# Experts' down weights: four neighbouring rows per partition instead of two, in a one-core transformer kernel

## What is computed

```
def expert_block(args):
    xb, e = args
    return (jax.nn.silu(xb @ w_gate[e]) * (xb @ w_up[e])) @ w_down[e]
...
y = ys[slot_of_assign].reshape(t, TOP_K, d)
out = jnp.einsum('tk,tkd->td', gates.astype(y.dtype), y)
```

## Time and profile before

| | |
|---|---|
| time, median of 3 runs | 1894.48 us (1893.77 to 1898.86) |
| profiled execution, first to last instruction (its span) | 1894.2 us |
| PE busy | 1833.4 us, 97% |
| PEld busy | 1524.4 us, 80% |
| DVE busy | 1469.6 us, 78% |
| ACT busy | 1213.1 us, 64% |
| moved by DMA | 511.54 MB, mean 270 GB/s |
| mean granted PE clock | 0.992 |

### The profile page before, as it was taken

One profiled execution on the slowest core, in us unless ns is written; L12 is line 12 of the kernel. 1 busy time (PEld: TensorE's weight loads), 2 busy tenths in 40 slices (PEclk: granted clock), 3 DMA queues, 4 the chain that ended last, 5 costly groups with the idle time before them and its releaser, 6 DMA issues.

```text
span 1894.2 us, 22429 instructions
## 1 busy us (share of the span) xinstructions
PE 1833.4 (97%) x9190; PEld 1524.4 (80%) x9190; DVE 1469.6 (78%) x1418; ACT 1213.1 (64%) x1258; POOL 142.4 (8%) x118
## 2 busy tenths in 40 slices
PE   7999999999999999999999999999999999999997
PEld 6888878888988788888788887878888787888875
DVE  5646565444579764458879899999989999998997
ACT  6555555433564454345637788988778898777784
POOL 2511100000100140004130000000000000000000
PEclk9999999999999999999989999999999999999999
DMA  8533345544442465344358999999999999999994
GB/s 296 177 134 134 134 154 204 198 178 151 170 169 89 156 224 198 134 160 154 131 202 342 373 354 423 420 422 420 395 363 362 419 420 422 418 379 368 370 420 167
DMA packets 154782, 511.54 MB, mean 270 GB/s; under 512 B 4431, under 2 KB 8898, under 8 KB 140338
## 3 DMA queue, kind: packets, MB, share of 16 engines
q1 hardware_dynamic: 152674, 504.53, 69.2%
q0 software_dynamic: 1392, 4.53, 0.7%
q10 hardware_dynamic: 608, 0.99, 0.1%
HBM read 508.98 MB, written 1.05 MB: 269 GB/s over the span
## 4 chain that ended last, share of the span: by engine, by line
PE 71%; DVE 17%; DMA 6%; ACT 3%; issue 2%; POOL 0%; ACTq 0%; SPq 0%; DVEq 0%; POOLq 0%
PE PS L442 19%; PE PS L444 19%; PE PS L443 19%; DVE WLX L1911 6%; DVE WLB L1911 6%; DMA ring<-in_moe_w_down 4%; PE PS L900 2%; PE PS L1139 1%; PE PS L1140 1%; ACT WHX L1290 1%; DMA ring<-in_moe_w_gate 1%; PE PS L1070 1%; PE PS L1072 1%; ACT WHB L1290 1%; PE PS L596 1%
## 5 line engine op out<-in xcount | busy, mean ns | idle before, releaser
L1911 DVE TENSOR_TENSOR WLB<-ring,WHB 128x2048 fp32r<-128x2048 f32 (+1 forms) x344 | 636.6, 1867 | 113.2 <-ACT WHB L1290 112.7
L1290 ACT ACTIVATE WHB<-ring 128x2048 fp32r<-128x2048 f32 (+1 forms) x344 | 531.5, 1557 | 300.1 <-PE PS L444 270.6
L1911 DVE TENSOR_TENSOR WLX<-ring,WHX 128x2048 fp32r<-128x2048 f32 (+1 forms) x216 | 469.1, 2192 | 51.2 <-ACT WHX L1290 51.0
L1290 ACT ACTIVATE WHX<-ring 128x2048 fp32r<-128x2048 f32 (+1 forms) x216 | 392.6, 1834 | 156.4 <-PE PS L444 124.8
L442 PE MATMUL PS<-WHB,XH 128*128 128x512 f32 (+1 forms) x640 | 255.2, 399 | 8.6 <-DVE XL L1945 2.4
L444 PE MATMUL PS<-WHB,XL 128*128 128x512 f32 (+1 forms) x640 | 247.7, 387 | 0.0
L443 PE MATMUL PS<-WLB,XH 128*128 128x512 f32 (+1 forms) x640 | 247.1, 386 | 0.0
L442 PEld LDWEIGHTS PS<-WHB,XH 128*128 128x128 f32 x640 | 121.1, 189 | 36.7 <-issue 6.2
L2831 POOL TENSOR_TENSOR SM<-SM,MH 128x8 f32<-128x8 f32 (+3 forms) x28 | 38.1, 1366 | 1392.1 <-DVE SM L1924 1392.1
L444 PEld LDWEIGHTS PS<-WHB,XL 128*128 128x128 f32 x640 | 120.8, 189 | 25.0
L443 PEld LDWEIGHTS PS<-WLB,XH 128*128 128x128 f32 x640 | 121.3, 190 | 21.8
(11 more groups left out here) (422 smaller groups left out, 3407.6 us busy)
## 6 DMA issues: line engine op xcount, KB each, us to landing
ring<-in_moe_w_gate SPq DMA_DIRECT2D x56, 2048.0 KB, 11.1
ring<-in_moe_w_up SPq DMA_DIRECT2D x56, 2048.0 KB, 10.9
ring<-in_moe_w_down SPq DMA_DIRECT2D x56, 2048.0 KB, 11.7
ring<-in_w_in SPq DMA_DIRECT2D x13, 2048.0 KB, 7.8
ring<-in_hg_w_in SPq DMA_DIRECT2D x8, 2048.0 KB, 8.4
ring<-in_da_w_in SPq DMA_DIRECT2D x6, 2048.0 KB, 7.9
ring<-in_w_gate SPq DMA_DIRECT2D x5, 2048.0 KB, 7.5
ring<-in_w_up SPq DMA_DIRECT2D x5, 2048.0 KB, 7.6
```

The costliest lines, as they stand in the source:

```text
L1290: e.activation(hi, src, ACT.Copy).then_inc(s_hi, 1)
L1911: e.tensor_tensor(lo, src, hi.bitcast(F32), ALU.subtract).then_inc(s_lo, 1)
```

## The change

Each down transfer now takes a chunk's 512 rows as 128 runs of four neighbouring rows (16 KB): partition p gets rows 4p to 4p+3. The transfer is still one instruction of 2 MB; its shape goes from 128x2x2048 to 128x4096. To match, group j of `inner` now holds the hidden columns 4n + j, so PE's weight loads in `expert_turn` read every fourth fp32 value, a step of 16 bytes. Each engine issues the same instructions in the same order, SP too.

```
@@ -1102,7 +1102,7 @@
             def inner(x, j):
 
-                return x.rearrange("p (a n b) -> p a b n", a=2, b=2)[:, j // 2, j % 2, :]
+                return x.rearrange("p (n b) -> p b n", b=4)[:, j, :]
 
             def expert_turn(ex, c):
@@ -2986,7 +2986,7 @@
                 w = w[bass.ds(T["expert", ex], 1)] if ex else w[0:1]
                 if kind == "down":
-                    return w.rearrange("o (a p b) n -> p (o a) (b n)", p=128, b=2)[:, at_ // 2:at_ // 2 + 2, :]
+                    return w.rearrange("o (a p b) n -> p (o a) (b n)", p=128, b=4)[:, at_ // 4:at_ // 4 + 1, :]
                 c0, k0 = at_
```

## The result

| | before | after |
|---|---|---|
| time, median of 4 runs | 1894.78 us | 1962.22 us (1960.6 to 1965.83) |
| span of the profiled execution | 1894.2 us | 1958.7 us |
| mean granted PE clock | 0.992 | 0.975 |

The change makes the kernel 67 us slower: the ratio is 1.0359, with a 95% interval of 1.0346 to 1.0371. I had forecast 1923 us, with a range from 1890 to 1941 us. The sign was right; the size, 28 us, was less than half of what came.

What follows compares the result with a forecast made beforehand. PE was taken to bound heavy experts, DVE and DMA light ones. Heavy turns 8.4 us plus light experts 20 us gave 28.4 us, with the transfers' gain hidden: 1923 us, range 1890 to 1941 us.

Steps and rivals of the forecast that it cites:

- What bounds: Expert stage: PE bounds heavy stretches; DVE and DMA together bound light experts, where PE has 8.6 us of room.
- room: PE's spare time per light expert: a period of 103.7 us less 95.1 us of PE work, 8.6 us.
- The transfers: Down transfers with 16 KB packets: 0.02 us gained each, 0.9 us over 35 light ones, hidden once PE bounds.
- The price of a pass in light turns: Weight loads at a 16-byte step: 0.100 us more per pass, 11.2 us of PE work per light expert.
- DVE's row at 32 bytes: DVE reduction of 64 values: 270 ns against 220 ns for neighbours, 0.78 ns a value, 100 ns for 128.
- DVE's row for 8 bytes: DVE at a step of 8 bytes or less lost nothing: 1234 ns against 1219 ns for 1024 values.
- full price: Rival on PE's turn loads: 61 ns for each further 4 bytes, 122 ns a pass, 1937 us; chance 0.13, or more included.
- Heavy turns: Heavy experts' turns on PE's path: 84 passes slowed by 0.100 us each, 8.4 us in all.
- Interlock: Light experts: 2.6 us of PE excess plus 1.4 us lost between PE and DVE, 4.0 us each, 20 us for five.

Runs made afterwards that it cites:

- half dose: The kernel before, with the 16-byte step for the up half of the light turns alone (280 of 560 passes): 1904.93 us, ratio 1.0045.
- wide turn: The changed kernel, with six of the eight products of a light turn passing 128 columns instead of 64: 1929.6 us, ratio 1.0183.

## Why the prediction fell short, step by step

- **What bounds.** Right. Heavy stretches hang on PE, light ones on DVE and the transfers. The chain after goes through PE (85% of the span), as I had said it would. The half dose bears out that there is room: 6 us of added PE work per light expert cost 8.5 us in five experts, not 30.
- **The transfers.** Right: nothing within 0.2%, 424 GB/s at 16 KB.
- **The price of a pass in light turns.** Right in size: 0.100 us taken, (3.61 - 1.89) / 16 = 0.108 us measured. That is luck. I took it from DVE's row at 32 bytes, one instruction of another engine, and no run here ties that to PE, whose loads rise with each 4 bytes (65 and 68 ns). DVE's row for 8 bytes was a weak witness too: of its eight instructions only the last, of 1.25 us, has that step. The "full price" rule of equal amounts for each further 4 bytes had the form right and the load's size nearly (318 ns against 329 ns), but not its premise that any slowing is paid in full since load and distance stand level: they stood at 196 and 118 ns, the load grew by 133 ns and the mean distance over a turn by 108.
- **Heavy turns.** Wrong: 8.4 us forecast, 0 measured (a turn of 0.48 us, not the 0.87 us I had named). I carried the product's price over to transposes. The 61 ns that a step of 8 bytes costs their loads grow by 3 ns at 16.
- **Interlock.** Too small: 4.0 us per light expert forecast. The wide turn, with the clock held, took 110.40 - 103.70 = 6.7 us; with 7 x 1.72 = 12.0 us of added work and 8.6 us of room, that is a loss of 3.3 us, not 1.4, if the room was 8.6 us. Over all light experts the wide turn took 35 us more than the kernel before, against my 20.
- **The step that failed: no term for PE's clock.** I added up PE's work with every product at 0.226 us, which is their distance at full clock, and gave no reason why the clock should hold with slower turns; no rival had it either. Behind 20 of 35 light turns it fell to 0.50 and the distance to the next product rose to 0.43 us. Measured: 33 us, the difference between the changed kernel and the wide turn. That alone carries the time out of the range; without it, at 1929.6 us, it lies inside. Even there the sum is close partly by luck, since the 8.4 us too much in heavy experts offset more than half of the 15 us too little in light ones.

In sum: 35 us by the turns' length (wide turn against the kernel before) and 33 us by the clock (changed kernel against wide turn), 0 in heavy experts, 0 by the transfers.

The rule of the Trainium skill on lines of 16 bytes (Advanced Engine Details and Errata, section Memory Cachelines) named the right danger: 8 bytes free, 16 bytes slow. Its mechanism doesn't match PE's loads here: by hits per line I had expected some 295 ns at 12 bytes, and the loads lie midway between those at 8 and 16, at 261 ns. Nor does it fit the transposes, whose loads pay at 8 bytes (140 to 201 ns) and hardly more at 16 (204 ns).

## What to carry to other kernels

When a layout is turned to suit a transfer, ask which engine has to read against the grain now, and at what width. Here a product's weight load on the matrix engine kept its pace up to 8 bytes between values and slowed by 65 and 68 ns for each 4 bytes beyond, up to the 16 bytes that were tried. An engine with 8% of room can be the bound after a small edit; and where PE gets slower at something in which it passes few columns, look at its granted clock behind it before adding up durations. A reorder is best put where it is free: here on the PSUM side of a copy that has to be made anyway.

## What the runs showed of the hardware

- PE fell to 1.2 GHz with no idle time before it: PE was busy 6.00 of 6.00 us from 1188 to 1194 us, and the clock was 0.50 from 1195 on. The Trainium skill (TensorE: Matmul & The Clock Gate, section Why this matters for your kernels) warns of idle gaps between bursts; here the clock fell behind 16 passes that each wait for a slow load and pass 64 columns. 128 columns in six of eight products, at the same pace, kept it at 1.00 and gave back 33 us; twice the passes at the old step, in a turn as long, held it at 1.00 too.
- Passing 128 columns instead of 64 behind a load of 329 ns costs nothing in pace (1.69 us for the first eight passes in both kernels).
- ACT pays for a step on the side of the on-chip buffer that it writes (512 bytes: 582 to 1114 ns for 512 values), and nothing for a step of 16 bytes on the PSUM side that it reads.
- Packets of 2, 4, 8 and 16 KB ran at 411, 421, 423 and 424 GB/s in this kernel: beyond 4 KB nearly nothing was left to gain.
